# Sums of weight blocks made ahead in DRAM by copying and accumulating DMAs, in place of GpSimd additions

## The reference, cut to what matters

```python
def sqrelu_mlp(hn, w1, w2):            # block 1, w1 is 1024 x 4096
    u = hn @ w1.astype(hn.dtype)
    u = jnp.square(jax.nn.relu(u))
    return u @ w2.astype(hn.dtype)
```

## Time and profile before

| | us |
|---|---|
| median of 3 runs (lowest, highest) | 2059.39 (2058.56, 2064.13) |
| the profiled execution | 2055.45 |
| its span | 2053.5 |
| TensorE busy / VectorE / ScalarE / GpSimd | 1970.8 / 1226.9 / 806.8 / 432.2 |

### The profile page before, as it was taken

How to read it: one execution, slowest core, us unless ns; L and a number is a source line. 1 busy time by engine, 2 the same in 40 slices (tenths; PEclk the granted TensorE clock), 3 DMA queues, 4 the chain that set the end, 5 groups by cost and what they waited for, 6 DMA issues and landing times.

```text
span 2053.5 us, 29329 instructions
## 1 busy us (share of the span) xinstructions
PE 1970.8 (96%) x11954; PEld 1717.1 (84%) x11954; DVE 1226.9 (60%) x1633; ACT 806.8 (39%) x1069; POOL 432.2 (21%) x312
## 2 busy tenths in 40 slices
PE   8999989999999999999999999999997899999996
PEld 6788766788888888999899999998884578888895
DVE  6668756656565654122566566556897557566565
ACT  4448734533232433223353232234434444233232
POOL 2012230202113220013222121212245122032122
PEclk9999999999999998999999999999998999999998
DMA  4223111123232221211123233223131022223231
GB/s 176 103 83 115 62 62 62 62 103 103 86 103 100 91 95 42 82 42 42 62 83 103 83 103 104 83 103 103 62 106 40 22 83 102 103 83 103 99 106 62
DMA packets 27850, 175.06 MB, mean 85 GB/s; under 512 B 4409, under 2 KB 4537, under 8 KB 7762
## 3 DMA queue, kind: packets, MB, share of 16 engines
q1 hardware_dynamic: 25680, 167.32, 23.6%
q0 software_dynamic: 1888, 5.90, 0.9%
q10 hardware_dynamic: 162, 0.10, 0.0%
HBM read 171.19 MB, written 4.78 MB: 86 GB/s over the span
## 4 chain that ended last, share of the span: by engine, by line
PE 72%; issue 12%; DVE 6%; POOL 4%; ACT 4%; DMA 2%; SPq 0%; POOLq 0%; DVEq 0%; ACTq 0%
PE lin L533 50%; PE lin L1833 6%; PE aux L1833 5%; POOL squares L752 2%; DMA w_raw<-in_weights 1%; PE aux L1425 1%; ACT w_hi L442 1%; PE aux L2645 1%; PE lin L1627 1%; PE lin L1380 1%; DVE w_lo L449 1%; PE lin L2615 1%; POOL w_lo L449 1%; PE aux L2629 1%; POOL r_t L2245 1%
## 5 line engine op out<-in xcount | busy, mean ns | idle before, releaser
L533 PE MATMUL lin<-x_hi,w_hi 128*128 128x512 f32 (+1 forms) x1160 | 408.8, 352 | 14.5 <-DVE tmp L628 6.5
L533 PE MATMUL lin<-x_hi,w_lo 128*128 128x512 f32 (+1 forms) x1160 | 407.0, 351 | 0.0
L533 PE MATMUL lin<-x_lo,w_hi 128*128 128x512 f32 (+1 forms) x1160 | 406.8, 351 | 0.0
L449 DVE TENSOR_TENSOR w_lo<-w_raw,w_hi 128x2048 fp32r<-128x2048 f32 (+1 forms) x118 | 276.3, 2341 | 176.4 <-ACT w_hi L442 175.6
L533 PE MATMUL lin<-v_hi,w_hi 128*128 128x264 f32 (+1 forms) x1088 | 365.3, 336 | 9.0 <-DVE tmp L1873 4.1
L533 PE MATMUL lin<-v_hi,w_lo 128*128 128x264 f32 (+1 forms) x1088 | 361.3, 332 | 0.0
L533 PE MATMUL lin<-v_lo,w_hi 128*128 128x264 f32 (+1 forms) x1088 | 360.9, 332 | 0.0
L442 ACT ACTIVATE w_hi<-w_raw 128x2048 fp32r<-128x2048 f32 (+1 forms) x129 | 242.8, 1882 | 206.2 <-PE lin L533 196.1
L533 PEld LDWEIGHTS lin<-x_hi,w_hi 128*128 128x128 f32 x1160 | 219.4, 189 | 49.5 <-DVE tmp L628 7.3
L533 PEld LDWEIGHTS lin<-x_hi,w_lo 128*128 128x128 f32 x1160 | 219.7, 189 | 29.9
L533 PEld LDWEIGHTS lin<-x_lo,w_hi 128*128 128x128 f32 x1160 | 219.5, 189 | 30.0 <-issue 0.2
(11 more groups left out here) (449 smaller groups left out, 3937.7 us busy)
## 6 DMA issues: line engine op xcount, KB each, us to landing
w_raw<-in_weights SPq DMA_DIRECT2D x155, 1024.0 KB, 4.8
rel_by_distance<-rel_by_distance POOLq DMA_DIRECT2D x1, 2599.5 KB, 20.3
rel_bias<-rel_by_distance POOLq DMA_DIRECT2D x8, 264.0 KB, 3.0
h<-in_x_t SPq DMA_DIRECT2D x4, 512.0 KB, 7.7
out_t<-h SPq DMA_DIRECT2D x4, 512.0 KB, 2.8
o_t<-in_mem_t POOLq DMA_DIRECT2D x1, 1024.0 KB, 4.9
cst<-in_consts SPq DMA_DIRECT2D x1, 512.0 KB, 9.3
col<-in_cols ACTq DMA_DIRECT2D x1, 67.0 KB, 5.5
```

Source lines behind the costliest of these rows:

```text
L449: does.tensor_tensor(w_lo[:, s, 0:n], w_raw[:, s, 0:n], w_hi[:, s, 0:n].bitcast(F32), ALU.subtract).then_inc(sem("w_lo_ready"), 1)
L533: last = nc.tensor.matmul(o, a, b, start=(k % (L.kc // k_banks) == 0 and p == 0), stop=((k + 1) % (L.kc // k_banks) == 0 and p == 2))
```

## The change

GpSimd adds no weight blocks any more. A DRAM tensor `w_sums` of 26 units is filled during the run by DMAs that GpSimd issues: first plain copies of the quad units (`pool_quad_base`), then accumulating DMAs in three dependent steps, `pool_quad_pairs` (two block sums), `pool_quad_triples` and `pool_quad_fours`, each of one DMA (pairs: two) per run of units with equal distance. There are three such runs in each of ff1, up0 and up1, so 9 copies, 18 pairs, 9 triples and 9 fours. The three groups' steps are placed in GpSimd's hand-written order, each with a wait for the step before. A quad unit is now loaded in three DMAs by `sp_unit`: three blocks of the original, the sum of two blocks that a product uses alone from `w_sums` in place of the fourth, and the three other sums into `w_sum`, so 1.75 MiB in place of 1 MiB. SyncE's loop is unrolled. [...] Blocks in a unit have another order. Products, columns and split widths are the same.

```diff
@@ -350,30 +350,78 @@
 
         quad_units = [L.unit0 + u for L in layer.values() for u in L.quads]
         quad_seq = {u: q for q, u in enumerate(quad_units)}
+        quad_layer = {L.unit0 + u: L.name for L in layer.values() for u in L.quads}
+
+        def runs_of(at):
+
+            if len({b - a for a, b in zip(at, at[1:])}) < 2:
+                return [at]
+            cuts = [0] + [x + 1 for x in range(len(at) - 1) if at[x + 1] > at[x] + 1] + [len(at)]
+            return [at[a:b] for a, b in zip(cuts, cuts[1:])]
+
+        SUM_RUNS = {group: [(name, run) for name in QUADS if name[0:3] == group for run in runs_of(QUADS[name])]
+                    for group in ("ff1", "up0", "up1")}
 
         def w_block(t, unit, a, b):
             return t[:, unit % 2, a * BLOCK_W:b * BLOCK_W]
 
-        def quad_sum(pool, unit, step):
-
-            q = quad_seq[unit]
-            a11, a12, a22, a21 = (w_block(w_raw, unit, x, x + 1) for x in range(4))
-            s3, s2, s4 = (w_sum[:, x * BLOCK_W:(x + 1) * BLOCK_W] for x in range(3))
-            if step == 0:
-                pool.wait_ge(sem(f"w_loaded{unit % 2}"), 16 * (unit // 2 + 1))
-                if q:
-                    pool.wait_ge(sem("w_lo_ready"), quad_units[q - 1] + 1)
+        def quad_rows(run, t, a, b):
+
+            units = [layer[run[0]].unit0 + u for u in run[1]]
+            if t is w_sums:
+                t = t[quad_seq[units[0]]:quad_seq[units[-1]] + 1]
             else:
-                pool.wait_ge(sem("quad_sum"), 4 * q + step)
-            out_t, x, y, op = ((s3, a21, a11, ALU.subtract), (a21, a21, a22, ALU.add),
-                               (s2, a21, a11, ALU.subtract), (s4, a12, s2, ALU.subtract))[step]
-            nc.gpsimd.tensor_tensor(out_t, x, y, op).then_inc(sem("quad_sum"), 1)
-
-        def pool_quad_sums(pool, *names):
-            for name in names:
-                for t in layer[name].quads:
-                    for step in range(4):
-                        quad_sum(pool, layer[name].unit0 + t, step)
+                t = t[units[0]:units[-1] + 1:units[1] - units[0] if len(units) > 1 else 1]
+            return t[:, :, a * BLOCK_W:b * BLOCK_W].rearrange("q p n -> p q n")
+
+        def sums_made(group):
+
+            return 16 * sum(len(SUM_RUNS[g]) for g in list(SUM_RUNS)[0:list(SUM_RUNS).index(group) + 1])
+
+        def pool_quad_base(pool, group, *parts):
+            for run in SUM_RUNS[group]:
+                if run[0][3] in parts:
+                    pool.dma_start(quad_rows(run, w_sums, 0, 4), quad_rows(run, weights, 0, 4))\
+                        .then_inc(sem("sum_base"), 16)
+
+        def pool_quad_pairs(pool, group):
+            pool.wait_ge(sem("sum_base"), sums_made(group))
+            for run in SUM_RUNS[group]:
+                pool.dma_start(quad_rows(run, w_sums, 3, 4), quad_rows(run, weights, 0, 1), accum_op=ALU.add)\
+                    .then_inc(sem("sum_pair"), 16)
+                pool.dma_start(quad_rows(run, w_sums, 0, 1), quad_rows(run, weights, 1, 2), accum_op=ALU.add)\
+                    .then_inc(sem("sum_pair"), 16)
+
+        def pool_quad_triples(pool, group):
+            pool.wait_ge(sem("sum_pair"), 2 * sums_made(group))
+            for run in SUM_RUNS[group]:
+                pool.dma_start(quad_rows(run, w_sums, 1, 2), quad_rows(run, w_sums, 3, 4), accum_op=ALU.add)\
+                    .then_inc(sem("sum_s2"), 16)
+
+        def pool_quad_fours(pool, group):
+            pool.wait_ge(sem("sum_s2"), sums_made(group))
+            if group != "ff1":
+                pool.wait_ge(sem("sum_s4"), sums_made(group) - 16 * len(SUM_RUNS[group]))
+            for run in SUM_RUNS[group]:
+                pool.dma_start(quad_rows(run, w_sums, 2, 3), quad_rows(run, w_sums, 1, 2), accum_op=ALU.add)\
+                    .then_inc(sem("sum_s4"), 16)
+
+        def sp_unit(sp, unit):
+
+            s, q = unit % 2, quad_seq.get(unit)
+            if unit > 1:
+                sp.wait_ge(sem("w_lo_ready"), unit - 1)
+            if q is None:
+                sp.dma_start(w_raw[:, s, :], weights[unit]).then_inc(sem(f"w_loaded{s}"), 16)
+                return
+            made = sums_made(quad_layer[unit][0:3])
+            sp.dma_start(w_raw[:, s, BLOCK_W:], weights[unit][:, BLOCK_W:]).then_inc(sem(f"w_loaded{s}"), 16)
+            sp.wait_ge(sem("sum_pair"), 2 * made)
+            sp.dma_start(w_raw[:, s, 0:BLOCK_W], w_sums[q][:, 3 * BLOCK_W:]).then_inc(sem("quad_s1"), 16)
+            if q:
+                sp.wait_ge(sem("w_lo_ready"), quad_units[q - 1] + 1)
+            sp.wait_ge(sem("sum_s4"), made)
+            sp.dma_start(w_sum[:, :], w_sums[q][:, 0:3 * BLOCK_W]).then_inc(sem("quad_sums"), 16)
 
         def quad_hi(act, unit, part, tiles_before):
 
@@ -381,17 +429,17 @@
             if part == 0:
                 act.wait_ge(sem("lin_done"), tiles_before)
                 act.wait_ge(sem(f"w_loaded{unit % 2}"), 16 * (unit // 2 + 1))
+                nc.scalar.activation(w_block(w_hi, unit, 1, 2), w_block(w_raw, unit, 1, 2), ACT.Copy)\
+                    .then_inc(sem("quad_w_hi"), 1)
+            elif part == 1:
+                nc.scalar.activation(w_block(w_hi, unit, 2, 4), w_block(w_raw, unit, 2, 4), ACT.Copy)\
+                    .then_inc(sem("quad_w_hi"), 1)
+            elif part == 2:
+                act.wait_ge(sem("quad_s1"), 16 * (q + 1))
                 nc.scalar.activation(w_block(w_hi, unit, 0, 1), w_block(w_raw, unit, 0, 1), ACT.Copy)\
                     .then_inc(sem("quad_w_hi"), 1)
-            elif part == 1:
-                nc.scalar.activation(w_block(w_hi, unit, 1, 3), w_block(w_raw, unit, 1, 3), ACT.Copy)\
-                    .then_inc(sem("quad_w_hi"), 1)
-            elif part == 2:
-                act.wait_ge(sem("quad_sum"), 4 * q + 2)
-                nc.scalar.activation(w_block(w_hi, unit, 3, 4), w_block(w_raw, unit, 3, 4), ACT.Copy)\
-                    .then_inc(sem("quad_w_hi"), 1)
             else:
-                act.wait_ge(sem("quad_sum"), 4 * q + 4)
+                act.wait_ge(sem("quad_sums"), 16 * (q + 1))
                 nc.scalar.activation(ws_hi[:, :], w_sum[:, :], ACT.Copy).then_inc(sem("w_hi_ready"), 1)
 
         def quad_lo(dve, unit, part):
@@ -402,7 +450,7 @@
                 nc.vector.tensor_tensor(ws_lo[:, :], w_sum[:, :], ws_hi[:, :].bitcast(F32), ALU.subtract)\
                     .then_inc(sem("w_lo_ready"), 1)
                 return
-            a, b = ((0, 1), (1, 3), (3, 4))[part]
+            a, b = ((1, 2), (2, 4), (0, 1))[part]
             dve.wait_ge(sem("quad_w_hi"), 3 * q + part + 1)
             nc.vector.tensor_tensor(w_block(w_lo, unit, a, b), w_block(w_raw, unit, a, b),
                                     w_block(w_hi, unit, a, b).bitcast(F32), ALU.subtract)\
@@ -704,11 +752,11 @@
         def dve_quad_sums(dve, N, j):
 
             t1, t4, t2, t3 = (vt_raw[:, x, j, 0:N.half] for x in range(4))
-            nc.vector.tensor_tensor(t1, h_half(N, j, 1), h_half(N, j, 0), ALU.subtract)
+            link(dve, nc.vector.tensor_tensor(t1, h_half(N, j, 1), h_half(N, j, 0), ALU.subtract))
             dve.wait_ge(sem("quad_gained"), N.quads0 + j + 1)
-            link(dve, nc.vector.scalar_tensor_tensor(t3, h_half(N, j, 1), N.gain(j), t3, ALU.mult, ALU.subtract))
-            link(dve, nc.vector.scalar_tensor_tensor(t2, h_half(N, j, 0), N.gain(j), t3, ALU.mult, ALU.subtract))
-            nc.vector.tensor_tensor(t4, t4, t2, ALU.subtract).then_inc(sem("quad_raw"), 1)
+            link(dve, nc.vector.scalar_tensor_tensor(t2, t1, N.gain(j), t3, ALU.mult, ALU.subtract))
+            nc.vector.scalar_tensor_tensor(t3, h_half(N, j, 1), N.gain(j), t3, ALU.mult, ALU.subtract)
+            nc.vector.tensor_tensor(t4, t4, t2, ALU.add).then_inc(sem("quad_raw"), 1)
 
         def dve_quad_operand(dve, N, j):
 
...
@@ -1863,7 +1911,7 @@
             unit, hf, n = L.unit0 + t, L.n // 2, L.n
             wait_product(dve, L, t, "p5")
             dve.wait_ge(sem("quad_top"), quad_seq[unit] + 1)
-            nc.vector.tensor_tensor(tmp[:, 0:2, hf:n], spread_row(tmp[:, 0, 0:hf]), lins[:, 1:3, 0:hf], ALU.add)\
+            nc.vector.tensor_tensor(tmp[:, 0:2, hf:n], spread_row(tmp[:, 0, 0:hf]), lins[:, 1:3, 0:hf], ALU.subtract)\
                 .then_inc(sem("quad_mid"), 1)
 
         def dve_quad_second_row(dve, L, t):
...
@@ -2884,13 +2929,8 @@
             sp.dma_start(cst[:, :, :], consts).then_inc(sem("consts_loaded"), 16)
             sp.dma_start(w_raw[:, 1, :], weights[1]).then_inc(sem("w_loaded1"), 16)
             sp.dma_start(h[:, :, 0:META], meta_t).then_inc(sem("meta_loaded"), 16)
-            with sp.Fori(1, n_units // 2) as i:
-                for s in range(2):
-                    sp.wait_ge(sem("w_lo_ready"), 2 * i + s - 1)
-                    sp.dma_start(w_raw[:, s, :], one_unit(2 * i + s)).then_inc(sem(f"w_loaded{s}"), 16)
-            if n_units % 2:
```

(22 more changed lines are left out.)

11 lines of the change are left out of this document (5 added, 6 removed).

## The result

The changed kernel takes 2068.17 us (median of 11 runs, 2066.76 to 2075.47), the kernel before on the same chip 2063.67 us (median of 11, 2056.60 to 2066.96). The ratio is 1.0043, its 95% interval 1.0026 to 1.0059; it goes by the means, 2070.82 and 2062.04 us, which are 8.8 us apart. The profiled execution of the changed kernel is one of 2068.17 us, with a span of 2066.2 us; that of before took 2055.45 us with a span of 2053.5. The two profiled executions are thus 12.7 us apart and the medians only 4.5.

The account below looks back on a forecast made before the run. TensorE, busy for 96% of the span, was taken as the bound. 2055.45 - 4.1 + 1.1 + 1.2 + 10.5 = 2064.2 us for the profiled execution; with 3.9 us to the median, 2068 us; range 2055 to 2088.

Parts of the forecast that it names:

- Quad gaps: up0 and up1 quad stretches: TensorE's second-row waits go with GpSimd's additions, -4.1 us; gain between 0 and 8.5.
- Loads and copies: Quad units loaded in three DMAs, and copies made ahead: weight loads stay in time, GpSimd's waits are covered; cost 0.
- Attention's start: Bias loads wait behind up1's fours on GpSimd's queue, so attention starts 10.5 us later; bounds 2.3 and 37.8 us.
- The gates: up0's fours ahead of the gate products: 2.4 us of issue less 1.3 of room, +1.1 us, between 0 and 2.4.
- The latent: up1's triples ahead of the latent's splits: 2.4 us of issue less 1.2 of room, +1.2 us, between 0 and 2.4.
- Held lightly: Rival, attention's start: accumulates at copy speed or bias loads not kept behind them, 0 to 2.3 us; 2055 to 2060; chance 0.3.
- All gaps close: Rival, quad stretches: all TensorE waits go and nothing is late at attention, -8.5 us, 2051 us; chance 0.1.
- Slow accumulates: Rival: accumulates take four copies' time or hold GpSimd several us each, +38 us, 2098 us; chance 0.15 shared with starved loads.
- Starved loads: Rival, up0's first quads: up1's copies delay weight loads past 19 us, some 5 us, 2078; chance 0.15 shared with slow accumulates.

Follow-up runs that it names:

- e9: Kernel before once more, unchanged, for a second profile; 2062.76 us.
- e10: Changed kernel once more, unchanged, for a second profile; 2068.93 us.
- e8: Changed kernel with GpSimd delayed by two small fills between issuing up0's step-four accumulates and the gates' products; 2067.63 us.
- e7: Changed kernel with up0's three step-four accumulates issued right behind its triples, ahead of GpSimd's gate-layer splits; 2068.86 us, ratio to before 1.0026.
- e4: Changed kernel with up1's three step-four accumulates as plain copies in the same place, the addition left out; 2073.96 us.
- e1: Changed kernel with up1's step-four accumulates issued behind the attention instead of ahead of its bias loads; 2057.8 us, ratio to before 0.9977.
- e5: Kernel before with GpSimd's weight-block additions replaced by fills, nothing for step one's; 2058.59 us, ratio to before 0.9973.
- e2: Changed kernel with up0's step four behind its triples and up1's pairs, triples and step four behind up1's copies; 2057.88 us, ratio to before 0.9965.
- e3: Changed kernel with the first two heads' bias loads issued from ScalarE's queue, accumulates left in place; 2061.42 us, a single time.
- e11: Changed kernel with up0's step four and up1's step three as plain copies in the same places, additions left out; 2067.71 us.
- e6: Kernel before with GpSimd delayed by four small fills ahead of the gates' products, no DMA added; 2063.27 us, ratio to before 0.9994.
- e12: Kernel before with six small fills on GpSimd ahead of the gates' products; 2061.57 us.

## Why the medians are closer than the profiles: e9 and e10

Both kernels once more, unchanged.

> The kernel before once more, for a second profile. In the first profile the attention, from VectorE's first masked logits to TensorE's last product with the values, took 81.2 us; in other kernels' profiles, in which no instruction of this part differs, it took 80.3 to 87.8, with a lower granted clock in its second half where it was long. Theory (this part's length varies from execution to execution and not by kernel): 85 us or more here, with a time of 2059 to 2064; all other parts within 1 us of the first profile. Rival (the kernel before has a short attention as such): 80 to 82 us, time 2055 to 2057.

> The changed kernel once more, for a second profile. Its eleven times lie in two groups, 2066.8 to 2068.2 and 2074.1 to 2075.5; the profiled one is of the first, with an attention of 80.3 us. Theory (the groups are short and long attentions of the same program): either 2066 to 2069 with 80 to 81 us, or 2073 to 2076 with 87 to 88 us, all other parts the same within 1 us. Rival (the groups come from another part, such as the accumulates' landing): in the long group the hold at the attention's start, 10.8 us, or the gates' 4.3 us differ.

The second execution of before took 2062.76 us, as the theory had it; everything outside the attention is within 0.9 us of the first, and the attention with "+" takes 97.8 us in place of 91.3. Windows over the attention, in the order before, before again, changed, up0's fours early (length, then busy us of TensorE, its weight loads, VectorE, ScalarE, GpSimd, then TensorE's granted clock):

```profile
1544.51:1625.67 81.16, 63.74 (x260) 37.53 (x258) 60.83 (x135) 40.74 (x112) 28.74 (x35) 0.89 0.07 21
```

```profile
1545.76:1631.77 86.01, 68.89 (x260) 39.60 (x259) 61.06 (x135) 40.75 (x112) 28.86 (x36) 0.84 0.07 19
```

```profile
1559.86:1640.15 80.29, 60.28 (x254) 35.66 (x255) 63.01 (x135) 40.60 (x111) 31.55 (x38) 0.89 0.07 21
```

```profile
1553.84:1641.24 87.40, 67.42 (x254) 38.82 (x254) 62.95 (x135) 40.58 (x111) 31.50 (x38) 0.81 0.07 19
```

VectorE, ScalarE and GpSimd do the same in the same time; only TensorE's busy time is longer, by 5 to 7 us, and its granted clock lower. Its last run of eight products with the values shows it best: 2.42 us before, 4.12 us in the second execution, with a granted clock of 1.00 (2.4 GHz) over the run there and of 0.59 here, that is mostly at the lower level of 1.2 GHz:

```profile
1625.67 2.42 PE L2645 MATMUL aux<-p_t,v_all 128*128 128x512 f32 x8
```

```profile
1631.77 4.12 PE L2645 MATMUL aux<-p_t,v_all 128*128 128x512 f32 x8
```

The granted clock shows where the two kinds part. It was read in steps of 5 us from VectorE's first masked logits. From 55 us on the first execution of before is at 1.00 throughout, and the changed kernel's (both, and e8's, step for step the same) but for one step of 0.66. The second execution of before is at 0.55 and 0.77 from 55 to 65 us and at 0.60 to 0.72 from 75 to 90; e7 and e4 fall at the same two places, to 0.54 to 0.78 and 0.50 to 0.84.

So the profiled execution of before had a short attention, which most of its runs seem not to have: of the 52 runs that stood beside the experiments with several rounds 4 are under 2056 us, and the medians were 2062.08 and 2064.99. The changed kernel's second execution (2068.93 us) had the short one again, as did e8. Its eleven times lie in two groups, 2066.8 to 2068.2 (six) and 2074.1 to 2075.5 (five), 7 us apart, about the distance between a short and a long attention in the table (6.5 us with "+" between the two executions of before, 8.8 between the changed kernel and e7); no execution of the upper group was traced, so this is an inference. So the changed kernel loses 13.6 us outside the attention; how much of it comes back inside depends on the executions compared: 0.9 us in the first pair of profiles, 7.4 in the second (97.84 - 90.43), 9 by the medians, 5 by the means.

What makes the attention short in one kernel and long in another **stays open**. The hold alone does not do it: e7 has the full hold and 87.4 us, e4 half of it and 87.8, e1 none and 84.3. Neither does a late gates stage, which e4 has too.

## Why the prediction was right, and where it was not

*Quad gaps.* Predicted -4.1 us; traced -4.6 (first pair of profiles) to -5.0 (second), and -3.1 to -5.6 over all four executions with additions. The cause, VectorE late behind GpSimd's additions, is shown by e5. The gate product's waits stayed at 3.5 us as said.

*Loads and copies.* Predicted 0, traced 0: 4.9 us for a load, and e2 has room for even more. GpSimd waited for up0's copies 28.7 us, with nothing due (33 us allowed).

*Attention's start.* Predicted +10.5 us, traced +10.8, and by the mechanism named: order in GpSimd's queue (e1, e3). Inside it two sizes were off against each other, and that they cancelled is luck: the accumulates took 13.6 us (1.6 copies, not 2, for 16.4 forecast), the bias loads 5.7 us from issue to use, for the 2.2 of the forecast. GpSimd's idle wait for the rows was the 14.3 us that "some 15" had named.

*The gates.* Predicted +1.1 with an upper bound of 2.4; traced +4.3. This term was mis-sized in three places. The issue was priced at 0.8 us, from plain DMAs; an accumulate holds GpSimd for 1.26 (e8, e11), so the delay was 3.8 and not 2.4. The slack of 1.3 us, read at VectorE's first scaling, was there at that instruction but only 0.2 at the end of the stage (e6, e12). And the exclusion of GpSimd and VectorE, read in the quad stage, was not applied to the place where GpSimd's work was moved: 0.6 to 0.7 us (e11). No row of before has a DMA issue right ahead of such products. The upper bound failed with the first of them, since no accumulate was in the trace and I bounded its transfer by four copies but its issue not at all.

*The latent.* Predicted +1.2 with an upper bound of 2.4; traced +2.0, by the same issue: 3.8 us of delay less a slack of 1.8, where 1.2 was read (e11: 2.3 us of delay cost 0.6).

*The sum and the median.* The terms gave +8.7 us on the profiled execution; traced were +12.7, or 13.6 outside the attention. The 3.9 us from the profiled execution to the median were taken over for the changed kernel; its profiled execution is its median, so they were 0 there, while before's median turned out to be 6.6 to 9.5 us above its profiled execution. The terms are too small by 4.0 and the offset too large by 3.9, and the forecast of 2068.0 meets 2068.17 by that coincidence. The 4.0 are 3.2 at the gates, 0.8 at the latent, 0.3 at the attention's start and 1.1 scattered, less 0.5 more gain in the quads and 0.9 inside the attention. The median itself is luck too: it is the highest of the six short runs, and with one of these six in the group of five it would have been 2074 us. What was right for its reasons is the sign, the place and two thirds of the size.

*The rivals.* Held lightly: excluded, the last accumulate landed at 1558.6 us, not by 1542, and the rows needed 16.95 us. All gaps close: the gaps nearly did close (0.9 us left of 4.2 in the middle windows), but the losses stayed. Slow accumulates: excluded by 1.6 copies and 1.26 us of issue. Starved loads: excluded by ScalarE's waits, 6.5 us in all.

## What to carry to other kernels

A DMA on a compute engine's queue can cost more than its issue: ask which small, urgent load is issued next on the same queue, and issue the bulk behind it or where the engine idles for long; here the same 45 DMAs are 16.6 us cheaper in other places, outside the attention. Bound the issue of a kind of DMA that the trace does not show as well as its transfer, and where GpSimd's work is moved next to VectorE's, count the exclusion too. Before a difference of 0.5% is read from two profiles, take a second profile of each: here a stretch of short TensorE bursts with waits between them differed by 6.5 us between two executions of one kernel, with a mean granted clock of 0.89 and 0.84 and nearly the same busy time on the other engines.

## What the runs showed of the hardware that I had not expected

- An accumulating DMA within DRAM held GpSimd for 1.26 us, a copy of the same form for 0.77, and the instruction behind either was recorded as started 0.77 us after the last issue. Three accumulates moved 2.62 MB in 13.6 us, three copies in 8.5 (both less the 5.66 us of the loads behind them).
- Seven GpSimd products directly behind a DMA issue left VectorE one turn, ahead of the last of them (product starts in e11), and its first two operations took 8.5 us in the changed kernel and e11 (the first of them 6.8 us in all six executions with that order); behind a split or a fill the two took 2.7 to 3.5 us.
- On a queue of its own a small load passed an accumulate that was issued 1.3 us ahead of it: 264 KB landed at 1548.8 us, the 768 KB accumulate at 1550.9 (e3). Behind three accumulates on GpSimd's queue it landed 0.6 us after the last of them.
- The attention, with no instruction changed, took 80.3 to 87.8 us, at a mean granted clock of 0.89 in the short and 0.81 to 0.84 in the long executions shown, with nearly the same busy time on the other engines.
